# x's high part and residual side by side: 512-column matmuls in the first block's feature slots

## The chip, the cores and the metric

The kernel runs on one NeuronCore of a Trainium2 chip, in one launch. The metric is the time of that launch on the device, in microseconds (us).
TensorE multiplies matrices: a block of up to 128x128 values stands still in the array (the weight load), and a moving operand of up to 512 columns is streamed past it; the result goes to PSUM, which has 8 banks of 512 float32 columns. ScalarE computes functions of one value (sigmoid, exp, copies), VectorE arithmetic on one or two tensors, GpSimd the same more slowly, and SyncE issues the DMAs. Each engine runs its own instructions in order and waits on semaphores for the others.

## The reference

Three blocks are computed in float32 on x of 256 tokens (T) by 2048 features: one of the first kind, which this change concerns, and two of a second kind. The first block:

```python
xn = rms_norm(x, norm_pre_w)
z = xn @ w_in                       # split in 8: u_lru, g_lru, q, k, v, g_attn, m_lru, m_attn
u = centred_depthwise_conv(u_lru, conv_w, conv_b)             # 4 taps
h = rg_lru(u, ..., reverse=False) + rg_lru(u, ..., reverse=True)
y_a = h * silu(g_lru)
y_b = windowed_gqa(partial_rope(q), partial_rope(k), v, sink) * silu(g_attn)
merged = sigmoid(m_lru) * (y_a @ w_proj_a) + sigmoid(m_attn) * (y_b @ w_proj_b)
x = x + rms_norm(merged @ w_out, norm_post_w)
# rg_lru: gate_r, gate_i = sigmoid(u @ w_r + b_r), sigmoid(u @ w_i + b_i) per block of 128 features,
# a = exp(-8 gate_r softplus(-lam)), h[t] = a[t] h[t-1] + sqrt(1 - a^2)[t] gate_i[t] u[t]
```

## The kernel before, in words

**Products in three terms.** TensorE's fast float32 format (fp32r) keeps fewer bits. Each operand is therefore held as a high part (rounded to the format) and a residual (the value less the high part), and a product is the sum hi*hi + hi*lo + lo*hi. For x these are `xn_hi` and `xn_lo`, two tensors of [128, 16 k-tiles, 256 tokens] (line 2955); for the weights, `w_hi` and `w_lo`.

**The ring of slots** (class `Ring`, line 246). The weights come as slots of 128 x 2048 values (1 MB), numbered in order of use. SyncE loads slot n into one of two raw buffers (`load`, 254; it waits until the slot two before it has been split). ScalarE rounds it to `w_hi` (`round`, 263; 4 buffers, so it also waits until slot n-4 has been used), and VectorE subtracts to get `w_lo` (`residual`, 272). TensorE then uses it, and `used` counts the slots done.

**Feature slots** (`features`, 297) give one tile of 128 features by 256 tokens: for each of 16 k-tiles the weights stand still and x moves, three matmuls of 256 columns, 48 a slot. The result fills half a PSUM bank, `tile(b)` (444). **Token slots** (`tokens`, 309) keep x still and stream 512 weight columns, 24 matmuls a slot.

**The first block's slots.** 0 to 31: eight passes of the LRU branch, four feature slots each (two of `u_lru`, into banks `z[0]` and `z[1]`, then two of `g_lru`, into `z[2]` and `z[3]`). 32 to 39: keys and values (token slots). 40 to 71: four attention chunks, each of four token slots (queries) and four feature slots (`g_attn`), so there are 48 feature slots. Then come token slots only.

**A pass i of the LRU branch.** TensorE runs slots 4i to 4i+3 and then the gate products `gates(i)` (1108): eight float32 products with the convolved u, two PSUM banks a feature tile. The other engines go through iterations 0 to 8 (lines 605 and 872); iteration i handles the inputs of pass i and the gates of pass i-1, with n = 4i. The order in each engine is the order of the program:

- ScalarE: `gate_inputs(i-1)` (556: sigmoid of `g_lru`), `gates(i-1)` (563: eight sigmoids of the gate products), round n+3, `tanhs(i-1)`, round n+4, `input_copy(i)` (593: PSUM to `padded`), `exps_lru(i-1)` with a square root, round n+5, round n+6, `round_y(i-1)` (601), which waits for `y`.
- VectorE: `open_gates(i-1)` (839: `g_lru` times its sigmoid, which also frees its bank), residual n+3, residual n+4, `convolve(i)` twice (825: four taps each), `scan(i-1)` (844), residual n+5, `outputs_lru(i-1)` (860: makes `y`), residual n+6, `split_y(i-1)`.
- GpSimd multiplies `gate_i` by u when the eight sigmoids are done.
- TensorE waits, ahead of slot 4i+b, for `input_copy(i-1, b)`, and ahead of slot 4i+2+b for `open_gates(i-1)`; ahead of `gates(i)` for the convolution and for the sigmoids of the pass before.

Iteration 0 has VectorE's softplus chain of small instructions at its end, iteration 2 the rotary angles.

**An attention chunk c.** After the query slots ScalarE copies them out and VectorE rotates them; TensorE transposes heads and computes scores between the four feature slots, VectorE (`soften`, 933) and ScalarE (`exps`) form the softmax in the same stretch, and ScalarE's `silu(c, j)` (665) takes feature slot j out of PSUM. TensorE waits for the `silu` two before to reuse a bank (1206 to 1210). The chunk's end is done during the next one (`finish_chunk`).

Of the kernel before, what the change touches and what calls it, by code (L numbers as in the profile page):

```python
# [245 lines left out]
class Ring:  # L246
# [61 lines left out]

    def tokens(self, pe, n, quarter, outs, x_hi, x_lo):
# [36 lines left out]
def reduce_angles(link, dve, angle, turns, rest, looked):  # L346
# [4 lines left out]
    for n, quarter in enumerate((0.0, 0.25)):  # L351
# [5 lines left out]
        for m, part in enumerate(turn_parts):  # L357
# [8 lines left out]
           "weights0 weights1 gated cleared chain exped ucopied conv gsig zcopied gates taken decay dsteps rounded_y ydone "  # L366
           "counted rotary_in rchain rlooked mask_in sink_in sinkready "
           "kcopied kroped kturned keyed vcopied qcopied roped qturned qevac scored0 scored1 soft0 soft1 "
           "exped0 exped1 flipped0 flipped1 fcopied0 fcopied1 mixed0 mixed1 yout0 yout1 yrounded0 yrounded1 ylo silued "
# [4 lines left out]
def first_block(k, t):  # L374
# [3 lines left out]
    with phase(nc, "b1", B1_SEMS) as s:  # L378
# [67 lines left out]

        def pair(c):
            return (z[2 * (c % 2)][:, 0:Q], z[2 * (c % 2) + 1][:, 0:Q])
# [10 lines left out]
        with nc.Block() as block:  # L459
# [55 lines left out]
            def _(act):  # L515
                act.wait_ge(s.eps, 1)
                act.activation(k.warm[:], k.eps[:], ACT.Sqrt)
                for h in range(2):
                    for m in range(2):
                        act.wait_ge(x_in[2 * m + h], 16)  # L520
                        act.activation(k.junk[:, half(m, m)], x_first[:, m, half(m, h)], ACT.Square, scale=D ** -0.5,
                                       accum_out=k.squares[:, m, h:h + 1]).then_inc(s.squared, 1)
# [142 lines left out]
                def silu(c, j):  # L665
# [3 lines left out]
                    act.activation(gate[:, j], tile(2 + j % 2), ACT.Silu).then_inc(s.silued, 1)  # L669

                def finish_chunk(c, n):

                    ring.round(act, n + 3)
# [3 lines left out]
                    if c >= 0:  # L677
                        copy_weights(c, 0)
                        silu(c, 3)
# [8 lines left out]
                for c in range(4):  # L688
# [10 lines left out]
                    for h in range(2):  # L699
                        act.wait_ge(s.qturned, 2 * c + h + 1)  # L700
                        act.activation(q_turned[:, 2 * h:2 * h + 2], both(aux[2 + h]), ACT.Copy).then_inc(s.qevac, 1)
                    ring.round(act, n + 8)
                    silu(c, 0)
                    ring.round(act, n + 9)
                    silu(c, 1)
                    silu(c, 2)
# [68 lines left out]
            def _(dve):  # L775
# [96 lines left out]
                for i in range(LRU_PASSES + 1):  # L872
                    n = 4 * i
                    if i:
                        open_gates(i - 1)
# [9 lines left out]
                    if i:  # L885
                        scan(i - 1)
# [74 lines left out]

                def open_heads(c, p):
# [10 lines left out]
                def finish_chunk(c, n):  # L973
                    if c >= 0:
                        normalise(c, 0)
                    ring.residual(dve, n + 3)
# [13 lines left out]
                for c in range(4):  # L990
# [5 lines left out]
                    ring.residual(dve, n + 7)  # L996
                    ring.residual(dve, n + 8)
                    soften(c, 0)
                    ring.residual(dve, n + 9)
                    soften(c, 1)  # L1000
                    ring.residual(dve, n + 10)
# [81 lines left out]
            def _(pe):  # L1083
# [41 lines left out]

                for i in range(LRU_PASSES):
                    for b in range(2):
                        if i:
                            pe.wait_ge(s.ucopied, 2 * (i - 1) + b + 1)
                            ring.features(pe, 4 * i + b, tile(b), k.xn_hi, k.xn_lo)  # L1130
                        else:
                            ring.features(pe, b, tile(b), k.xn_hi, k.xn_lo, (first_rows, second_rows)[b], False)
# [1932 lines left out]
```

## Time and profile before

| | |
|---|---|
| median of 3 runs | 1992.32 us (1991.84 to 1992.9) |
| the profiled execution | 1995.17 us, its span 1993.4 us |
| TensorE busy | 1935.8 us (97%), 13840 matmuls |
| VectorE busy | 1265.2 us (63%) |
| ScalarE busy | 1104.7 us (55%) |
| mean granted TensorE clock | 0.996 of full speed |
| feature matmuls of 256 columns (line 306, all three blocks) | 3 x 2112 |
| token matmuls of 512 columns (line 318, weights moving) | 3 x 568 with xn, 3 x 368 with y |

The span is the time between the first and the last instruction; the metric has 1.8 us more around it. Times in a view count from the start of the span. A busy share is an average over the whole program; what one stage is bound by is read from the waits and the order of events in that stage. A matmul's recorded duration is longer than the distance between two starts, since matmuls overlap in the array: distances of starts are what they cost.

### The profile page before, as it was taken

The page shows a single profiled execution, that of the slowest core. Times are in us where ns is not written, and L with a number is a line of the kernel's source. Part 1 is how long each engine was busy: PE and PEld are TensorE (multiplying, and loading weights), DVE is VectorE, ACT ScalarE, POOL GpSimd, SP SyncE. Part 2 cuts the span into 40 slices and gives each one's busy share as a digit, 9 for nine tenths or more (in the row PEclk, how much of TensorE's full clock was granted, in tenths as well). Part 3 has the DMA queues.
Part 4 walks back from the last instruction along what each step waited for, and adds up shares of the span by engine and source line. Part 5 has one row for each costly group of instructions (what it writes and reads, how often), then busy time and mean ns, then how long its engine had stood idle before and what let it go on. Part 6 is the DMA issues. An engine that isn't in the chain of part 4 may idle for free.

```text
span 1993.4 us, 32637 instructions
## 1 busy us (share of the span) xinstructions
PE 1935.8 (97%) x13840; PEld 1726.6 (87%) x13840; DVE 1265.2 (63%) x1771; ACT 1104.7 (55%) x1506; POOL 70.1 (4%) x66
## 2 busy tenths in 40 slices
PE   6999999999999999999899999999999999999998
PEld 6999989999888888888798988888889998988887
DVE  5878755555444434654587987555557899775453
ACT  6777745554433333334556578826455656883451
POOL 0111100000000000000000011100000001010000
PEclk9999999999999999999999999999999999999999
DMA  6444454444455555464544343312555444342154
GB/s 226 183 183 183 166 205 160 161 152 143 175 175 205 190 187 190 178 250 169 208 172 149 146 166 112 141 70 104 212 194 208 168 157 140 128 148 86 64 191 148
DMA packets 52272, 328.61 MB, mean 165 GB/s; under 512 B 7968, under 2 KB 10144, under 8 KB 14368
## 3 DMA queue, kind: packets, MB, share of 16 engines
q1 hardware_dynamic: 52128, 326.54, 45.5%
q8 instruction: 109, 1.79, 0.3%
q14 instruction: 35, 0.29, 0.1%
HBM read 320.23 MB, written 6.29 MB: 164 GB/s over the span
## 4 chain that ended last, share of the span: by engine, by line
PE 26%; DVE 11%; ACT 8%; DMA 5%; issue 2%; SPq 0%; DVEq 0%; ACTq 0%
PE z L306 13%; DMA w_raw<-in_w_dram 5%; DVE w_lo L277 4%; PE z L318 4%; ACT w_hi L270 3%; PE aux L2683 2%; DVE acc L2006 2%; DVE conv L2164 1%; PE z L342 1%; PE aux L2592 1%; PE aux L2688 1%; PE z L2521 1%; DVE S L2120 0%; PE aux L2767 0%; DVE S L2145 0%
## 5 line engine op out<-in xcount | busy, mean ns | idle before, releaser
L277 DVE TENSOR_TENSOR w_lo<-w_raw,w_hi 128x2048 fp32r<-128x2048 f32 x274 | 631.3, 2305 | 445.2 <-ACT w_hi L270 444.6
L270 ACT ACTIVATE w_hi<-w_raw 128x2048 fp32r<-128x2048 f32 x286 | 548.1, 1918 | 506.2 <-PE z L318 246.5
L306 PE MATMUL z<-xn_hi,w_hi 128*128 128x256 f32 x2112 | 621.7, 294 | 2.7 <-DVE xn_lo L234 1.5
L306 PE MATMUL z<-xn_hi,w_lo 128*128 128x256 f32 x2112 | 596.4, 282 | 0.0
L306 PE MATMUL z<-xn_lo,w_hi 128*128 128x256 f32 x2112 | 595.6, 282 | 0.0
L306 PEld LDWEIGHTS z<-xn_hi,w_hi 128*128 128x128 f32 x2112 | 398.8, 189 | 22.3 <-issue 13.4
L306 PEld LDWEIGHTS z<-xn_lo,w_hi 128*128 128x128 f32 x2112 | 399.5, 189 | 5.0 <-issue 4.3
L306 PEld LDWEIGHTS z<-xn_hi,w_lo 128*128 128x128 f32 x2112 | 397.9, 188 | 0.0
L318 PE MATMUL z<-w_hi,xn_hi 128*128 128x512 f32 x568 | 226.9, 399 | 0.0
L318 PE MATMUL z<-w_lo,xn_hi 128*128 128x512 f32 x568 | 225.2, 396 | 0.0
L318 PE MATMUL z<-w_hi,xn_lo 128*128 128x512 f32 x568 | 225.1, 396 | 0.0
L318 PE MATMUL z<-w_hi,y_hi 128*128 128x512 f32 x368 | 143.6, 390 | 0.0
L318 PE MATMUL z<-w_hi,y_lo 128*128 128x512 f32 x368 | 143.3, 389 | 0.0
L318 PE MATMUL z<-w_lo,y_hi 128*128 128x512 f32 x368 | 143.2, 389 | 0.0
L318 PEld LDWEIGHTS z<-w_hi,xn_lo 128*128 128x128 f32 x568 | 107.0, 188 | 26.1
L318 PEld LDWEIGHTS z<-w_hi,xn_hi 128*128 128x128 f32 x568 | 107.0, 188 | 25.4
L318 PEld LDWEIGHTS z<-w_lo,xn_hi 128*128 128x128 f32 x568 | 107.0, 188 | 25.3
L2006 DVE SCALAR_TENSOR_TENSOR acc<-padded_b,params,acc 128x256 f32<-128x256 f32 x240 | 98.5, 478 | 0.0
L318 PEld LDWEIGHTS z<-w_hi,y_lo 128*128 128x128 f32 x368 | 69.1, 188 | 14.3
L318 PEld LDWEIGHTS z<-w_hi,y_hi 128*128 128x128 f32 x368 | 69.1, 188 | 14.2
L2164 DVE SCALAR_TENSOR_TENSOR conv<-padded,params,conv 128x256 f32<-128x256 f32 x108 | 58.1, 538 | 36.7 <-ACT conv L1738 34.1
L318 PEld LDWEIGHTS z<-w_lo,y_hi 128*128 128x128 f32 x368 | 69.1, 188 | 14.1
(428 smaller groups left out, 2527.9 us busy)
## 6 DMA issues: line engine op xcount, KB each, us to landing
w_raw<-in_w_dram SPq DMA_DIRECT2D x287, 1024.0 KB, 4.8
gate_w<-in_lru_w_dram SPq DMA_DIRECT2D x8, 512.0 KB, 5.6
x_t<-state_dram SPq DMA_DIRECT2D x2, 2048.0 KB, 8.3
x_first<-in_x_dram SPq DMA_DIRECT2D x4, 512.0 KB, 6.5
x_t<-in_x_dram SPq DMA_DIRECT2D x1, 2048.0 KB, 10.6
state_dram<-x_t SPq DMA_DIRECT2D x2, 1024.0 KB, 5.3
pw<-in_pw_dram SPq DMA_DIRECT2D x2, 1024.0 KB, 6.6
state_dram<-x_t SPq DMA_DIRECT2D x8, 256.0 KB, 2.3
```

The costliest lines, as they stand in the source:

```text
L270: act.activation(self.k.w_hi[:, n % SLOTS], self.k.w_raw[:, m % RAW], ACT.Copy).then_inc(self.s.rounded, 1)
L277: dve.tensor_tensor(self.k.w_lo[:, n % SLOTS], self.k.w_raw[:, m % RAW], self.k.w_hi[:, n % SLOTS].bitcast(F32), ALU.subtract).then_inc(se ...
L306: ins = pe.matmul(out, w[:, kk], x[:, kk], start=kk == 0 and j == 0, stop=kk == KT - 1 and j == 2)
L318: ins = pe.matmul(outs[m], x[:, row, t], w[:, kk], start=row == 0 and j == 0, stop=row == KT - 1 and j == 2)
L342: ins = pe.matmul(outs[m], x[:, row, t], w[:, kk], start=row == 0 and j == 0, stop=row == KT - 1 and j == 2)
L2006: dve.scalar_tensor_tensor(out=acc[:, b], in0=padded_b[:, b, n:n + T], scalar=col(w), in1=acc[:, b], op0=ALU.mult, op1=ALU.add).then_inc(s ...
L2164: dve.scalar_tensor_tensor(out=conv[:, i], in0=padded[:, i, tap:tap + T], scalar=col(w), in1=conv[:, i], op0=ALU.mult, op1=ALU.add).then_i ...
L2521: ins = pe.matmul(z[3][0:2 * H, 0:T], w[:, kk], x[:, kk], start=kk == 0 and i == 0, stop=kk == KT - 1 and i == 2)
L2592: ins = pe.matmul(aux[m // 2][:, T * (m % 2):T * (m % 2) + T], pw[:, b, P * m:P * m + P], wide[:, b], start=b == 0, stop=b == B - 1)
L2683: ins = pe.matmul(block(bank, h, hf), left[part_of(hf), h], right[part_of(hf), h], start=True, stop=True)
L2688: ins = pe.matmul(block(bank, h, hf), x[part_of(hf), h], ident_c[part_of(hf)], start=True, stop=True)
```

## The change

Three things change together.

1. `xn_hi` and `xn_lo` become views of one tensor `xn` of [128, 16, 2, 256], so that for each k-tile the high part and the residual of x lie side by side. In the 48 feature slots of the first block, `wide_features` streams both in one matmul of 512 columns against `w_hi`, into a whole bank, and then 256 columns of the high part against `w_lo`, into the bank's first half: 32 matmuls a slot. The bank then holds hi*hi + lo*hi in its first half and hi*lo in the second (`rest`).
2. The two halves have to be added. ScalarE copies the first half out (`take_gates`, `take_gate`, the `input_copy` that was there), VectorE adds the second half from PSUM (`join_gates`, `join_gate`, a join at the head of `convolve`), and sigmoid and silu read the sum in SBUF. TensorE waits for the joins where it waited for the copies.
3. TensorE's `gates(i)` moves from the end of pass i into the first slot of pass i+1, ahead of its seventh k-tile (for the last pass, behind the first key slot). ScalarE's sigmoids move behind round n+3, VectorE's `open_gates` from the head of the iteration to between the convolution and the scan.

`junk` and `x_whole`, scratch that lies in the same memory, get the same interleaved form. The two blocks behind use the old `features` on the new layout.

```diff
+    def wide_features(self, pe, n, bank, x, each=None, whole=True):
+        w_hi, w_lo = (w[:, n % SLOTS].rearrange("p (k f) -> p k f", k=KT) for w in (self.k.w_hi, self.k.w_lo))
+        out = bank[:, 0:2 * T]
+        if whole:
+            self.await_slot(pe, n)
+        for kk in range(KT):
+            if each is not None:
+                each(kk)
+            row = x[:, kk].rearrange("p b t -> p (b t)")
+            if kk < KT - 1:
+                pe.matmul(out, w_hi[:, kk], row, start=kk == 0, stop=False)
+            ins = pe.matmul(out[:, 0:T], w_lo[:, kk], x[:, kk, 0], start=False, stop=False)
+            if kk == KT - 1:
+                ins = pe.matmul(out, w_hi[:, kk], row, start=False, stop=True)
+        ins.then_inc(self.s.used, 1)
...
+                def take_gates(i):                                        # ScalarE
+                    act.wait_ge(s.used, 4 * i + 4)
+                    if i:
+                        act.wait_ge(s.dsteps, 8 * i)
+                    for b in range(2):
+                        act.activation(g_all[:, b], tile(2 + b), ACT.Copy).then_inc(s.gtaken, 1)
                 def gate_inputs(i):
-                    act.wait_ge(s.used, 4 * i + 4)
                     if i:
                         act.wait_ge(s.zcopied, 2 * i)
                     for b in range(2):
-                        act.activation(gsig[:, b], tile(2 + b), ACT.Sigmoid).then_inc(s.gsig, 1)
+                        act.wait_ge(s.gjoined, 2 * i + b + 1)
+                        act.activation(gsig[:, b], g_all[:, b], ACT.Sigmoid).then_inc(s.gsig, 1)
...
                     if i:
-                        gate_inputs(i - 1)
-                        gates(i - 1)
+                        take_gates(i - 1)
                     ring.round(act, n + 3)
                     if i:
+                        gates(i - 1)
+                        gate_inputs(i - 1)
                         tanhs(i - 1)
...
-                def silu(c, j):
+                def take_gate(c, j):
                     act.wait_ge(s.used, SLOT_ATT + 8 * c + 4 + j + 1)
                     if c:
                         act.wait_ge(yout[j // 2], c)
-                    act.activation(gate[:, j], tile(2 + j % 2), ACT.Silu).then_inc(s.silued, 1)
+                    act.activation(gate[:, j], tile(2 + j % 2), ACT.Copy).then_inc(s.ataken, 1)
+                def silu(c, j):
+                    act.wait_ge(s.ajoined, 4 * c + j + 1)
+                    act.activation(gate[:, j], gate[:, j], ACT.Silu).then_inc(s.silued, 1)
...
                 def convolve(i, b):                                       # VectorE
                     dve.wait_ge(s.ucopied, 2 * i + b + 1)
+                    inner = padded[:, b, 2:2 + T]
+                    dve.tensor_tensor(inner, rest(b), inner, ALU.add).then_inc(s.ujoined, 1)
+                    dve.wait_ge(s.ujoined, 2 * i + b + 1)
...
+                def join_gates(i):
+                    for b in range(2):
+                        dve.wait_ge(s.gtaken, 2 * i + b + 1)
+                        dve.tensor_tensor(g_all[:, b], rest(2 + b), g_all[:, b], ALU.add).then_inc(s.gjoined, 1)
                 def open_gates(i):
                     dve.wait_ge(s.gsig, 2 * i + 2)
+                    dve.wait_ge(s.gjoined, 2 * i + 2)
                     for b in range(2):
-                        dve.tensor_tensor(g_all[:, b], tile(2 + b), gsig[:, b], ALU.mult).then_inc(s.zcopied, 1)
+                        dve.tensor_tensor(g_all[:, b], g_all[:, b], gsig[:, b], ALU.mult).then_inc(s.zcopied, 1)
...
                     if i:
-                        open_gates(i - 1)
+                        join_gates(i - 1)
                     ring.residual(dve, n + 3)
...
                         convolve(i, 1)
                     if i:
+                        open_gates(i - 1)
                         scan(i - 1)
...
+                def join_gate(c, j):
+                    dve.wait_ge(s.ataken, 4 * c + j + 1)
+                    dve.tensor_tensor(gate[:, j], rest(2 + j % 2), gate[:, j], ALU.add).then_inc(s.ajoined, 1)
...
+                def last_gates(kk, i):                                    # TensorE
+                    if kk == 6:
+                        gates(i)
...
-                            pe.wait_ge(s.ucopied, 2 * (i - 1) + b + 1)
-                            ring.features(pe, 4 * i + b, tile(b), k.xn_hi, k.xn_lo)
+                            pe.wait_ge(s.ujoined, 2 * (i - 1) + b + 1)
+                        if i:
+                            ring.wide_features(pe, 4 * i + b, z[b], k.xn, None if b else lambda kk: last_gates(kk, i - 1))
...
-                            pe.wait_ge(s.zcopied, 2 * (i - 1) + b + 1)
-                        ring.features(pe, 4 * i + 2 + b, tile(2 + b), k.xn_hi, k.xn_lo)
-                    gates(i)
-
-                pe.wait_ge(s.ucopied, 2 * LRU_PASSES)
+                            pe.wait_ge(s.gjoined, 2 * (i - 1) + b + 1)
+                        ring.wide_features(pe, 4 * i + 2 + b, z[2 + b], k.xn)
+                pe.wait_ge(s.ujoined, 2 * LRU_PASSES)
                 for w in range(4):
                     ring.tokens(pe, SLOT_K + w, w, pair(0), k.xn_hi, k.xn_lo)
+                    if w == 0:
+                        gates(LRU_PASSES - 1)
...
-        k.xn_hi, k.xn_lo = (put(n, [P, KT, T], F32R) for n in ("xn_hi", "xn_lo"))
+        k.xn = put("xn", [P, KT, 2, T], F32R)
+        k.xn_hi, k.xn_lo = k.xn[:, :, 0], k.xn[:, :, 1]
```

In the attention chunks ScalarE's `take_gate(c, j)` stands where `silu(c, j)` stood or ahead of the next round (j = 3 moves to the head of `finish_chunk`), silu 0 and 1 follow round n+9, silu 2 and 3 follow `copy_weights(c, 0)`; VectorE's `join_gate` stands behind residual n+7, `soften(c, 0)`, `soften(c, 1)` and `normalise(c, 0)`. TensorE waits for the joins.

## Rows read from the trace of the kernel before

**Rows 1.** Waits, 0 to 262 us: who waited for whom, total us, times, longest.

```profile
PE aux L1116 <- DVE u_all L835: 1.5, 1, 1.5
ACT y_hi L603 <- DVE y L865: 34.2, 7, 5.0
```

**Rows 2.** Timeline, TensorE, pass 1's end: start, us, instruction, operands.

```profile
65.80 0.28 PE L306 MATMUL z<-xn_lo,w_hi 128*128 128x256 f32 x1
...
71.80 3.62 PE L1116 MATMUL aux<-u_all,gate_w 128*128 128x256 f32 x16
75.07 0.47 PE L306 MATMUL z<-xn_hi,w_hi 128*128 128x256 f32 x1
```

**Rows 3.** Timeline, TensorE, in value slot 37.

```profile
263.19 0.39 PE L318 MATMUL z<-w_hi,xn_hi 128*128 128x512 f32 x1
...
268.11 0.38 PE L1149 MATMUL aux<-ident,q_tok 128*128 128x128 f32 x2
```

**Rows 4.** Timeline, TensorE, the gate products of pass 7.

```profile
230.92 3.62 PE L1116 MATMUL aux<-u_all,gate_w 128*128 128x256 f32 x16
```

**Rows 5.** Timeline, ScalarE, iteration 4, and two later roundings of y; idle in brackets.

```profile
133.29 0.63 ACT L603 ACTIVATE y_hi<-y 128x512 fp32r<-128x512 f32 x1 [5.03 <-DVE y L865]
133.94 1.28 ACT L561 ACT_TABLE_LOAD   x1
...
143.83 0.71 ACT L599 ACTIVATE padded<-z 128x256 f32<-128x256 f32 x2
144.56 1.28 ACT L588 ACT_TABLE_LOAD   x1
...
148.88 1.06 ACT L591 ACTIVATE tau<-tau 128x1024 f32<-128x1024 f32 x1
...
158.57 0.63 ACT L603 ACTIVATE y_hi<-y 128x512 fp32r<-128x512 f32 x1 [5.04 <-DVE y L865]
...
183.86 0.63 ACT L603 ACTIVATE y_hi<-y 128x512 fp32r<-128x512 f32 x1 [4.50 <-DVE y L865]
```

**Rows 6.** Timeline, VectorE, iteration 4.

```profile
135.98 0.75 DVE L842 TENSOR_TENSOR g_all<-z,gsig 128x256 f32<-128x256 f32 x2
140.64 2.94 DVE L277 TENSOR_TENSOR w_lo<-w_raw,w_hi 128x2048 fp32r<-128x2048 f32 x1 [3.91 <-ACT w_hi L270]
...
146.24 0.41 DVE L831 TENSOR_SCALAR u_all<-padded,params 128x256 f32<-128x256 f32 x1
146.68 1.53 DVE L835 SCALAR_TENSOR_TENSOR u_all<-padded,params,u_all 128x256 f32<-128x256 f32 x3
148.12 0.41 DVE L831 TENSOR_SCALAR u_all<-padded,params 128x256 f32<-128x256 f32 x1
...
150.01 1.22 DVE L848 SCALAR_TENSOR_TENSOR tau<-decay,tau 128x1024 f32<-128x1024 f32 x1
```

**Rows 7.** Timelines, iterations 0 and 1 (VectorE, ScalarE), and the DMA issues.

```profile
45.08 2.28 DVE L277 TENSOR_TENSOR w_lo<-w_raw,w_hi 128x2048 fp32r<-128x2048 f32 x1
...
59.33 1.71 ACT L581 ACTIVATE tau<-gate_r,scale_t 128x256 f32<-128x256 f32 x4 [3.18 <-DVE scale_t L906]
...
62.75 0.63 ACT L599 ACTIVATE padded<-z 128x256 f32<-128x256 f32 x2
...
w_raw<-in_w_dram SPq DMA_DIRECT2D x287, 1024.0 KB, 4.8
```

**Rows 8.** Timelines, iteration 8 and the keys: VectorE, ScalarE, VectorE.

```profile
255.44 2.27 DVE L277 TENSOR_TENSOR w_lo<-w_raw,w_hi 128x2048 fp32r<-128x2048 f32 x1
...
259.14 0.63 ACT L603 ACTIVATE y_hi<-y 128x512 fp32r<-128x512 f32 x1 [4.88 <-DVE y L865]
...
263.22 0.29 DVE L922 TENSOR_TENSOR q_tok<-rope_a,rope_b 128x128 f32<-128x128 f32 x1
```

**Rows 9.** Stretch of 48 us in the attention chunks (engine busy, count), and VectorE's softmax start.

```profile
358.00:406.00 48.00, 48.00 (x315) 43.94 (x314) 27.48 (x41) 26.19 (x41) 0.00 (x0) 1.00 0.46 166
...
317.03 1.29 DVE L936 SCALAR_TENSOR_TENSOR S<-aux,mask 128x512 f32<-128x512 f32 x2 [2.71 <-PE aux L1164]
```

More of the change, by code:

```diff
@@ L445, in tile, with rest @@
             return z[n][:, 0:T]
+        def rest(n):
+            return z[n][:, T:2 * T]
         def pair(c):
@@ L520, in _ @@
                         act.wait_ge(x_in[2 * m + h], 16)
-                        act.activation(k.junk[:, half(m, m)], x_first[:, m, half(m, h)], ACT.Square, scale=D ** -0.5,
+                        act.activation(k.junk[:, 4 * m:4 * m + 4], x_first[:, m, half(m, h)].rearrange("p (j t) -> p j t", t=T), ACT.Square, scale=D ** -0.5,
                                        accum_out=k.squares[:, m, h:h + 1]).then_inc(s.squared, 1)
@@ L678, in finish_chunk @@
                         copy_weights(c, 0)
+                        silu(c, 2)
                         silu(c, 3)
@@ L701, in _ @@
                         act.activation(q_turned[:, 2 * h:2 * h + 2], both(aux[2 + h]), ACT.Copy).then_inc(s.qevac, 1)
+                    take_gate(c, 0)
                     ring.round(act, n + 8)
+                    take_gate(c, 1)
+                    ring.round(act, n + 9)
                     silu(c, 0)
-                    ring.round(act, n + 9)
                     silu(c, 1)
-                    silu(c, 2)
+                    take_gate(c, 2)
                     ring.round(act, n + 10)
@@ L975, in finish_chunk @@
                         normalise(c, 0)
+                        join_gate(c, 3)
                     ring.residual(dve, n + 3)
@@ L996, in _ @@
                     ring.residual(dve, n + 7)
+                    join_gate(c, 0)
                     ring.residual(dve, n + 8)
                     soften(c, 0)
+                    join_gate(c, 1)
                     ring.residual(dve, n + 9)
                     soften(c, 1)
+                    join_gate(c, 2)
                     ring.residual(dve, n + 10)
@@ L1151, in turn_heads @@
                             ins.then_inc(out_sem, 1)
-                pe.wait_ge(s.zcopied, 2 * LRU_PASSES)
+                pe.wait_ge(s.gjoined, 2 * LRU_PASSES)
                 for w in range(4):
@@ L1208, in _ @@
                         else:
-                            pe.wait_ge(s.silued, 4 * c + j - 1)
-                        ring.features(pe, n + 4 + j, tile(2 + j % 2), k.xn_hi, k.xn_lo)
+                            pe.wait_ge(s.ajoined, 4 * c + j - 1)
+                        ring.wide_features(pe, n + 4 + j, z[2 + j % 2], k.xn)
                         if j == 0:
@@ L1225, in _ @@
                     if c == 1:
-                        pe.wait_ge(s.silued, 16)
+                        pe.wait_ge(s.ajoined, 16)
                     elif c:
@@ L1607, in scalar @@
             after(act, s.squared_x, since.squared_x + m)
-            act.activation(k.junk[:, 0:Q if layer else D], x, ACT.Square, scale=D ** -0.5, accum_out=total).then_inc(s.squared_x, 1)
+            act.activation(k.junk[:, 0:2 if layer else D // T], x.rearrange("p (j t) -> p j t", t=T), ACT.Square, scale=D ** -0.5, accum_out=total).then_inc(s.squared_x, 1)
         act.wait_ge(s.averaged, since.averaged + 1)
@@ L1929, in square @@
                 act.wait_ge(s.added, since.added + 2 * c + m + 1)
-                act.activation(k.junk[:, (2 * c + m) % 4 * Q:(2 * c + m) % 4 * Q + Q], x_t[:, m, cols(c)], ACT.Square, scale=D ** -0.5,
+                here = slice(2 * ((2 * c + m) % 4), 2 * ((2 * c + m) % 4) + 2)
+                act.activation(k.junk[:, here], x_t[:, m, cols(c)].rearrange("p (j t) -> p j t", t=T), ACT.Square, scale=D ** -0.5,
                                accum_out=k.squares[:, m, c:c + 1])
@@ L2954, in build @@
         k.middle = goto(k.xn_at)
-        k.xn_hi, k.xn_lo = (put(n, [P, KT, T], F32R) for n in ("xn_hi", "xn_lo"))
+        k.xn = put("xn", [P, KT, 2, T], F32R)
+        k.xn_hi, k.xn_lo = k.xn[:, :, 0], k.xn[:, :, 1]
         goto(k.xn_at)
-        k.junk = put("junk", [P, D])
-        goto(k.xn_at + 4 * KT * T)
-        k.x_whole = put("x_whole", [P, KT, T])
+        k.junk = put("junk", [P, KT, 2, T])[:, :, 0]
+        goto(k.xn_at)
+        k.x_whole = put("x_whole", [P, KT, 2, T])[:, :, 1]
         k.raw_at = k.middle + 4096
```

8 lines of the change are left out of this document (5 added, 3 removed).

## The prediction

> **What bounds the kernel now.** I read the page's busy times first: TensorE is busy 97% of the span, so the time moves only if TensorE's instructions get shorter or its waits change. Next I read the waits of the stage that the change touches, up to 262 us. Once TensorE has its first slots it waits there once, for 1.5 us, before the first pass's gate products [rows 1]; in the passes and in the attention chunks it runs without a gap. ScalarE, however, waits in seven of the eight iterations for `y` of VectorE, 34.2 us in all [rows 1]. Two clocks run side by side. TensorE's passes come every 26.5 us: the gate products of pass 1 start at 71.80 and those of pass 7 at 230.92, six passes in 159.1 [rows 2, 4]. ScalarE and VectorE hand work back and forth in a closed loop, from one rounding of `y` to the next: 133.29 to 158.57 is 25.28 us, and to 183.86 it is 25.29 again [rows 5]. That loop is only 1.2 us shorter than TensorE's pass. This margin decides the case.
>
> **The matmuls.** In a feature slot, 50 matmuls of 256 columns take from 65.80 to 71.80, 0.120 us apart [rows 2]; in a token slot, 21 of 512 columns take from 263.19 to 268.11, 0.2343 apart [rows 3]. A slot is 48 x 0.120 = 5.76 us now. Changed it is 16 x (0.2343 + 0.120) = 5.67, so 0.09 less. The column count (12,288) is unchanged and only 16 starts disappear. Bounds: no gain if the columns of a feature slot cost what they do now; 0.13 us if all run at the token slots' rate (12,288 x 0.2343/512 = 5.62). I take 0.09. For 48 slots that is 4.3 us at most.
> The Trainium skill (TensorE: Matmul & The Clock Gate, "Wait — 56ns, not 53.3ns?") speaks against more: a matmul costs its columns plus some 2.5 ns, so 16 fewer starts would be an estimate of 0.04 us a slot, under 2 us for 48. The measured starts differ by 2 x 120 - 234.3 = 5.7 ns, more than that, and the sum goes by the rows.
>
> **The gate products** cost 3.27 us before and after (71.80 to 75.07 [rows 2]); they only move to the seventh k-tile of the next pass's first slot. TensorE's own pass becomes 26.5 - 4 x 0.09 = 26.1 us. The four slots of pass 0 save nothing, as their ends hang on the first splits.
>
> **The ScalarE/VectorE loop, where the price is.** Its legs now [rows 5, 6]: ScalarE from rounding `y` (133.29) through table load, two sigmoids of the gate input, eight gate sigmoids, round of slot n+3, tanhs and round of slot n+4 to 143.83; VectorE's residual of slot n+4, 2.4 with its hand-over; the convolution 146.24 to 150.01, 3.77 us; scans, residual n+5, outputs, and back to ScalarE at 158.57, 8.56 us. The order inside ScalarE's leg changes but its work stays (the same number of table loads, since Copy needs none). Added to the loop:
> - ScalarE's two copies of the gate input (`take_gates`): as the two `padded` copies, 143.83 to the next start at 144.56, 0.73; I take 0.72.
> - VectorE's two joins inside `convolve`, each followed by a wait for itself. The nearest are the two `g_all` multiplies, same operands, 0.75 for both [rows 6], so 0.34 a start without a wait, and the three waited taps, 146.68 to 148.12, 0.48 each. I take 0.45 each, 0.90.
> - `open_gates`, moved from the stretch in which VectorE then idled 3.91 us [rows 6] to between convolution and scan: two multiplies, 0.70 (0.62 to 0.75).
> - The joins of the gate inputs take the old place of `open_gates`, in that idle stretch: nothing, while VectorE waits there for ScalarE.
> Could the ScalarE side hide VectorE's 1.60? Its decays and square root run 143.83 to 149.94 (148.88 + 1.06 [rows 5]), VectorE reaches the scan at 150.01. The two legs are level already, so all of VectorE's addition lands. The loop becomes 25.28 + 0.72 + 0.90 + 0.70 = 27.6 us (bounds 27.2 to 27.8), against TensorE's 26.1. So the loop, which lagged nobody, sets the pace: TensorE will wait 1.5 us in every pass.
>
> **Adding it up.** Iteration 1 is special: its tanhs wait for VectorE's softplus chain until 59.33, and round n+4 ends at 62.75 [rows 7]. In the changed order the sigmoids come behind round n+3, which needs slot 7, whose load needs slot 5's residual: 45.08, plus two joins 0.9, plus 2.2 of residual, plus 4.8 of load [rows 7] is 53.0. From there the same five items as in ScalarE's leg (133.94 to 143.83, 9.9 us [rows 5]) lead to 62.9; its tanhs then start near 59.5, so the chain no longer matters. With 0.90 and 0.70 behind it, the `y` of iteration 1 is 1.8 late (1 to 3). Iterations 2 to 7 add 2.3 each, 13.9. Iteration 8 has no convolution and waits for the square root, so it adds only the copies, 0.7. The last `y`, now at 259.14, comes 16.4 later, at 275.5.
> What TensorE needs from it [rows 8]: the residual of slot 37 ends (255.44 + 2.2) 1.5 before the last `y`, so at 274.0, and slot 37 (5.63) ends at 279.6. The rotated keys, now done at 263.5, 4.4 after the last `y`, come at 279.9, and the key transposes start then, where they started at 268.11. TensorE is 11.8 us late. The other 4.6 of the 16.4 are slack that the keys have now (263.5 to 268.11). Nothing behind gives it back, for TensorE runs there without gaps.
> In the attention chunks ScalarE is busy 26.2 and VectorE 27.5 us of 48 [rows 9]. Four copies and four joins a chunk (3 us) fit. The tightest is the second join, behind `soften`: that starts at 317.03 with 1.29 us for two products [rows 9] and a reduction over their results, an estimate of 3 us; the slot that reuses the bank starts a whole slot, 5.7 us, after the scores. If one were late, it costs tenths. So the 16 gate slots there give their 16 x 0.09 = 1.4 us.
> The strided halves of `xn`, `junk` and `x_whole` keep runs of 256 columns and change no count; I cost them at nothing (VectorE and ScalarE have idle time; each full pass over `xn` is a few instructions).
> Sum: +11.8 - 1.4 = +10.4. The profiled execution took 1995.17 (span 1993.4 and 1.8 around it), so 2005.6; the median of the runs is 2.85 lower, so **2002.7 us**.
>
> **Rivals.**
> - *TensorE keeps the pace (faster).* It wins if the loop grows by less than about 0.8 us a pass: 1.2 of margin, and the starting slack, cover that. The joins and `open_gates` would have to hide. For it: TensorE's passes have no gap now, and round n+3 now comes ahead of the sigmoids, some 4 us sooner after `y`. Against: that round stays in ScalarE's leg, only its place changes. Price: 44 x 0.09 = 4.0, plus the 1.5 before the first gate products: 1992.3 - 5.4 = 1986.9. Chance 0.08.
> - *Only ScalarE's copies lengthen the loop* (VectorE's additions fall beside decays that prove slower from the new order). Loop 26.0, level with TensorE: the last `y` is some 5 late (7 x 0.72), the slack takes 4.6, TensorE is about 1 late, and the attention slots give 1.4: 1992. Against: the two legs end 0.07 apart. Chance 0.07.
> - *More than the loop.* TensorE now stops inside an open slot for the convolution (the gate products' wait) and ends late; if its late slots then hold the rounds (which wait for a used slot) the two add up instead of overlapping, 1 us a pass more: 2010. Against: with the loop in the lead, round n+4 finds its slot free 14 us early. Chance 0.05.
> - *The wide matmul is no cheaper than its columns* (no gain in the attention slots): 2004.1. This lies inside the forecast's own spread.
>
> **How the numbers follow.** The forecast has 0.80. Its own range: 0.25 us a pass on six passes, 1 us of iteration 1, 1.4 of the matmuls, 1999 to 2006. A measurement of this kernel tells 0.2% (4 us) from nothing. The middle rival and the small edge of the forecast give "within" 0.09, the first rival gives "faster" 0.08, the rest is slower, 0.83. The range for 8 in 10 takes in the forecast with both bounds of the prices and a little on the low side: 1997 to 2008.
>
> **What would show it.** In the changed profile: wide matmuls 0.234 and narrow 0.120 apart, slots 5.67; roundings of `y` 27.6 us apart in iterations 3 to 7, with no idle time on VectorE between convolution, `open_gates` and scan; TensorE waiting once or twice a pass, for `w_lo` of slot 4i+5 (behind the scan) and for the convolution inside slot 4i+4, 1.5 us together; the gate products of successive passes 27.6 apart; the key transposes near 280; from there on, TensorE 12 to 10 us behind the old times. I am wrong if passes stay 26.1 apart, if ScalarE reaches the square root later than VectorE the scan, or if the attention chunks show new waits.

## The result, and the profile after

The changed kernel takes 2018.26 us (median of 4 runs, 2017.18 to 2021.67) against 1992.61 for the kernel before in the same comparison (1991.84 to 1993.7). The ratio is 1.0121, with a 95% interval of 1.0109 to 1.0134: slower by 25.7 us (the quotient of the two medians, 1.0129, lies inside the interval). The forecast, 2002.7 us, had the direction, but its increase was 10.4, and the time lies 10 us above its range. The profiled execution took 2021.67 us with a span of 2019.9, 26.5 more than the span before.

Each fence below is from the changed kernel unless its sentence says otherwise. The page's busy times first (share of the span, and number of instructions):

```profile
PE 1946.7 (96%) x13072; PEld 1695.4 (84%) x13072; DVE 1276.6 (63%) x1819; ACT 1116.7 (55%) x1538; POOL 69.5 (3%) x66
```

TensorE has 768 matmuls fewer and is yet busy 10.9 us longer than before, at a mean granted clock of 0.988 against 0.996; and the time in which it does nothing grew from 57.6 to 73.2 us. The waits of TensorE up to 300 us, which answer to [rows 1] (who waited for whom: us in total, times, longest; the 12.8 us until the first x is there, 12.9 before, are left out):

```profile
PE aux L1171 <- DVE u_all L875: 8.4, 6, 2.0
PE z L335 <- DVE w_lo L277: 5.4, 2, 4.3
PE z L320 <- DVE g_all L882: 2.7, 1, 2.7
PE z L320 <- DVE w_lo L277: 2.2, 3, 1.1
PE z L335 <- DVE padded L865: 2.0, 1, 2.0
PE z L320 <- DVE padded L865: 1.1, 2, 0.6
```

L1171 is the gate products, now inside a slot, and they wait for the convolution as forecast. The same view of ScalarE, 0 to 300 us:

```profile
ACT y_hi L630 <- DVE y L911: 44.2, 7, 6.6
ACT w_hi L270 <- DMA w_raw<-in_w_dram: 33.6, 15, 4.5
```

Before, the second row read 20.7 us in 11 waits in the same window. That row is the part that the forecast did not have. The timeline of ScalarE over one iteration shows where it sits (start, duration, instruction; in brackets the idle time before it and what ended it). It answers to [rows 5]:

```profile
171.62 0.63 ACT L630 ACTIVATE y_hi<-y 128x512 fp32r<-128x512 f32 x1 [6.61 <-DVE y L911]
172.16 0.64 ACT L581 ACTIVATE g_all<-z 128x256 f32<-128x256 f32 x2
174.96 1.92 ACT L270 ACTIVATE w_hi<-w_raw 128x2048 fp32r<-128x2048 f32 x1 [2.16 <-DMA w_raw<-in_w_dram]
176.89 1.28 ACT L596 ACT_TABLE_LOAD   x1
...
183.28 1.95 ACT L270 ACTIVATE w_hi<-w_raw 128x2048 fp32r<-128x2048 f32 x1
185.09 0.68 ACT L626 ACTIVATE padded<-z 128x256 f32<-128x256 f32 x2
...
190.11 1.06 ACT L618 ACTIVATE tau<-tau 128x1024 f32<-128x1024 f32 x1
...
201.40 0.64 ACT L630 ACTIVATE y_hi<-y 128x512 fp32r<-128x512 f32 x1 [6.62 <-DVE y L911]
```

From one rounding of `y` to the next is 29.78 us, not 27.6. Behind the two copies of the gate input ScalarE stands still for 2.16 us: the round of slot n+3 at 174.96, which the change put ahead of the sigmoids, has no data yet. VectorE's timeline over the same stretch (answers to [rows 6]) shows why:

```profile
167.93 2.27 DVE L277 TENSOR_TENSOR w_lo<-w_raw,w_hi 128x2048 fp32r<-128x2048 f32 x1
170.11 0.68 DVE L908 TENSOR_TENSOR gate_r<-gate_r 128x512 f32<-128x512 f32 x1
170.90 0.69 DVE L911 TENSOR_TENSOR y<-gate_r,g_all 128x512 f32<-128x512 f32 x1
...
176.91 2.29 DVE L277 TENSOR_TENSOR w_lo<-w_raw,w_hi 128x2048 fp32r<-128x2048 f32 x1 [1.85 <-ACT w_hi L270]
185.26 2.29 DVE L277 TENSOR_TENSOR w_lo<-w_raw,w_hi 128x2048 fp32r<-128x2048 f32 x1 [6.06 <-ACT w_hi L270]
187.47 0.42 DVE L865 TENSOR_TENSOR padded<-z,padded 128x256 f32<-128x256 f32 x1
...
192.16 0.75 DVE L888 TENSOR_TENSOR g_all<-g_all,gsig 128x256 f32<-128x256 f32 x2
192.83 1.22 DVE L894 SCALAR_TENSOR_TENSOR tau<-decay,tau 128x1024 f32<-128x1024 f32 x1
```

The residual of slot n+1 at 167.93 is the last reader of one of the two raw buffers. The load of slot n+3 goes out when it ends: SyncE issues it at 170.22, and with the 4.8 us of a load [rows 7] it lands at 175.0. Before the change the same round stood behind the sigmoids, 5.3 us behind `y`, and found its data there. Everything else in the loop is as forecast: the convolution with its joins is 4.69 us (187.47 to 192.16), 0.92 more than before; `open_gates` holds VectorE 0.67; and VectorE has no gap from 185.26 to `y`.

Last, TensorE at the end of the stage, first the timeline, then granted clock and busy times by window (us, engines with their counts, PEclk, share and GB/s of the DMA); they answer to [rows 3, 8]:

```profile
284.24 0.39 PE L335 MATMUL z<-w_hi,xn 128*128 128x512 f32 x1
288.93 0.79 PE L335 MATMUL z<-w_hi,xn 128*128 128x512 f32 x1 [4.30 <-DVE w_lo L277]
289.52 0.63 PE L335 MATMUL z<-w_lo,xn 128*128 128x512 f32 x1
...
297.05 0.40 PE L335 MATMUL z<-w_hi,xn 128*128 128x512 f32 x1
297.29 1.03 PE L1210 MATMUL aux<-ident,q_tok 128*128 128x128 f32 x8
```

```profile
284.00:288.00 4.00, 0.63 (x3) 0.19 (x1) 3.97 (x6) 1.33 (x1) 0.00 (x0) 0.99 0.00 0
288.00:292.00 4.00, 3.07 (x7) 2.48 (x8) 3.90 (x4) 1.60 (x3) 0.00 (x0) 0.50 0.46 158
292.00:298.00 6.00, 6.00 (x25) 4.78 (x24) 4.90 (x11) 2.54 (x2) 0.00 (x0) 0.77 0.78 288
```

The last `y` is rounded at 290.31, 31.2 later than before. Slot 37 waits 4.30 us for its residual and then takes 8.36 us (288.93 to 297.29) where it took 5.63, because TensorE comes out of that wait at half clock (0.50 granted, the 1.2 GHz level). The key transposes start at 297.29, 29.2 later than before.

### The profile page after: what moved, and what is told of

Its sections match the earlier page's. It is cut to its first block, busy times and chain, and to the rows that moved or that the text cites. A ratio compares the mean times of both kernels' runs of the same rounds, so it can differ in the third digit from the quotient of the medians.

```text
span 2019.9 us, 31201 instructions
## 1 busy us (share of the span) xinstructions
PE 1946.7 (96%) x13072; PEld 1695.4 (84%) x13072; DVE 1276.6 (63%) x1819; ACT 1116.7 (55%) x1538; POOL 69.5 (3%) x66
## 4 chain that ended last, share of the span: by engine, by line
PE 27%; DVE 11%; ACT 7%; DMA 4%; issue 2%; SPq 0%; DVEq 0%; ACTq 0%
PE z L306 14%; DMA w_raw<-in_w_dram 4%; PE z L335 4%; DVE w_lo L277 4%; ACT w_hi L270 3%; PE aux L2745 2%; DVE acc L2068 2%; DVE conv L2226 1%; PE z L359 1%; PE aux L2654 1%; PE aux L2750 1%; PE z L2583 1%; DVE S L2207 0%; PE aux L2829 0%; DVE S L2182 0%
## 5 line engine op out<-in xcount | busy, mean ns | idle before, releaser
L306 PE MATMUL z<-xn,w_hi 128*128 128x256 f32 x2688 | 512.8, 290 | 2.0 <-DVE xn L234 2.0
L306 PEld LDWEIGHTS z<-xn,w_hi 128*128 128x128 f32 x2688 | 416.9, 189 | 25.4 <-issue 17.1
L306 PE MATMUL z<-xn,w_lo 128*128 128x256 f32 x1344 | 379.8, 283 | 0.0
L335 PE MATMUL z<-w_hi,xn 128*128 128x512 f32 x1136 | 367.3, 401 | 7.4 <-DVE w_lo L277 5.4
L320 PE MATMUL z<-xn,w_hi 128*128 128x512 f32 x720 | 262.5, 403 | 6.1 <-DVE g_all L882 2.7
L335 PEld LDWEIGHTS z<-w_hi,xn 128*128 128x128 f32 x1136 | 216.0, 190 | 60.6 <-DVE w_lo L277 4.7
L306 PEld LDWEIGHTS z<-xn,w_lo 128*128 128x128 f32 x1344 | 253.4, 189 | 0.0
L335 PE MATMUL z<-w_lo,xn 128*128 128x512 f32 x568 | 226.7, 399 | 0.0
L321 PE MATMUL z<-xn,w_lo 128*128 128x256 f32 x768 | 207.9, 281 | 0.0
L320 PEld LDWEIGHTS z<-xn,w_hi 128*128 128x128 f32 x720 | 136.2, 189 | 38.9 <-DVE g_all L882 3.1
L321 PEld LDWEIGHTS z<-xn,w_lo 128*128 128x128 f32 x768 | 145.3, 189 | 3.8
L335 PEld LDWEIGHTS z<-w_lo,xn 128*128 128x128 f32 x568 | 108.2, 190 | 25.7
```

What stands on the lines that cost most here:

```text
L306: ins = pe.matmul(out, w[:, kk], x[:, kk], start=kk == 0 and j == 0, stop=kk == KT - 1 and j == 2)
L320: pe.matmul(out, w_hi[:, kk], row, start=kk == 0, stop=False)
L321: ins = pe.matmul(out[:, 0:T], w_lo[:, kk], x[:, kk, 0], start=False, stop=False)
L335: ins = pe.matmul(outs[m], x[:, row, t], w[:, kk], start=row == 0 and j == 0, stop=row == KT - 1 and j == 2)
```

## The experiments

All are edits of the changed kernel unless said otherwise. "Late" is the start of the key transposes less the 268.11 of before [rows 3]; ratios are to the kernel before in the same comparison.

| run | ratio (95%) | roundings of `y` apart | last `y` | late |
|---|---|---|---|---|
| the change | 1.0121 (1.0109 to 1.0134) | 29.8 | 290.31 | 29.2 |
| e1 round n+3 behind the gates | 1.0056 (1.0041 to 1.0071) | 27.5 | 276.92 | 14.7 |
| e2 `open_gates` early | 1.0094 (1.0077 to 1.0111) | 29.1 | 286.42 | 24.2 |
| e3 gate products at pass end | 1.0112 (1.0097 to 1.0127) | 29.8 | 288.65 | 24.9 |
| e4 wide in attention only | 1.0003 (0.9991 to 1.0015) | 25.3 | 259.50 | 0.8 |
| e5 both orders | 1.0032 (1.0021 to 1.0042) | 26.8 | 272.91 | 9.1 |
| e6 no joins for the convolution | 0.9993 (0.9983 to 1.0003) | 25.9 | 266.72 | 4.5 |
| m1 convolution in the idle stretch | 1.0089 (1.0074 to 1.0104) | 30.2 to 30.6 and 26.2 to 27.2, in turn | 283.60 | 19.8 |
| m2 as m1, copies ahead of `y`'s rounding | 1.0093 (1.0078 to 1.0108) | 31 and 26, in turn | 285.25 | 21.5 |
| b1 wide for gate inputs only | 0.9982 (0.9973 to 0.9991) | 25.35 | 260.26 | -0.4 |
| b2 all wide, copies in idle time | 0.9997 (0.9988 to 1.0006) | 26.3 | 266.19 | 2.4 |

**e1: one line moved back.** My theory after seeing the trace: the early round of slot n+3 costs its wait for the load, in every iteration. The rival: this round is only where the delay shows, and the loop would be as long without it.

```
-                    ring.round(act, n + 3)
-                    if i:
                         gates(i - 1)
                         gate_inputs(i - 1)
+                    ring.round(act, n + 3)
+                    if i:
                         tanhs(i - 1)
```

> ScalarE's round of slot n+3 goes back behind the gate sigmoids and the sigmoid of the gate input; all else as changed. Theory A (the closed loop of ScalarE and VectorE sets the pace; the forecast missed that round n+3, now 1.3 us after y, meets a load that lands only 3.3 us after y, since the load waits for a residual that ends 1.5 us before y): roundings of y 27.6 us apart instead of 29.8, no wait of round n+3 for the DMA, last rounding near 276, key transposes near 280, time 2001 to 2004. Rival B (TensorE's own stops, above all the wait for the convolution inside an open slot and the lower clock behind it, carry the loss): at most 2 to 4 us gained, 2014 to 2018.

The loop fell to 27.48 us, the last `y` to 276.92 and the ratio to 1.0056; half of the loss is gone. ScalarE's timeline in e1:

```profile
168.40 0.63 ACT L630 ACTIVATE y_hi<-y 128x512 fp32r<-128x512 f32 x1 [6.47 <-DVE y L911]
168.94 0.64 ACT L581 ACTIVATE g_all<-z 128x256 f32<-128x256 f32 x2
169.60 1.28 ACT L596 ACT_TABLE_LOAD   x1
...
174.38 1.96 ACT L270 ACTIVATE w_hi<-w_raw 128x2048 fp32r<-128x2048 f32 x1
177.78 1.94 ACT L270 ACTIVATE w_hi<-w_raw 128x2048 fp32r<-128x2048 f32 x1
...
195.88 0.63 ACT L630 ACTIVATE y_hi<-y 128x512 fp32r<-128x512 f32 x1 [6.61 <-DVE y L911]
```

The round at 174.38, now 6.0 us behind the rounding of `y`, waits for nothing. The theory stands, and this kernel is close to the one that the forecast had priced (27.6; last `y` 275.5; transposes 279.9, measured 282.81). The time, 2007.25 us, is above the 2001 to 2004 expected: the transposes come 2.9 us later than priced, and slot 37 takes 7.27 us here instead of 5.63. One interval is 28.2; in it the round of slot n+4 waited 0.62 us for its load.

**e2: `open_gates` alone.** It tests the price of the moved multiplies, and whether VectorE's side sets the loop at all.

```
+                    if i:
+                        open_gates(i - 1)
                     ring.residual(dve, n + 4)
```

(and the call behind the convolution goes.)

> VectorE's open_gates ahead of residual n+4, in the stretch where it waits for ScalarE; all else as changed. Theory A: 0.67 us out of the loop in seven iterations, 29.1 apart, last rounding near 286, time 2013 to 2015. Rival B: y is not what the end hangs on, no change, 2017 to 2019.

The loop became 29.1, 0.7 less: the two multiplies count in full. But the kernel is still 1.0094, so this was not the large term.

**e3: the gate products back at the end of their pass.** The rival here was my own "more than the loop": TensorE stopping inside an open slot.

```
-                            ring.wide_features(pe, 4 * i + b, z[b], k.xn, None if b else lambda kk: last_gates(kk, i - 1))
+                            ring.wide_features(pe, 4 * i + b, z[b], k.xn)
...
                         ring.wide_features(pe, 4 * i + 2 + b, z[2 + b], k.xn)
+                    gates(i)
```

> TensorE's gate products back at the end of their own pass; all else as changed, wide slots and joins too. Theory A: the loop stays at 29.8, for the sigmoids of the gates come later than the products either way; TensorE waits 5 us a pass in one piece at the gate products instead of 2 us inside the slot; time 2018 to 2021. Rival B: without the stop inside the slot 8 us of waits go, 2008 to 2012.

TensorE's waits up to 262 us in e3:

```profile
PE aux L1171 <- DVE u_all L875: 18.3, 7, 3.8
PE aux L1148 <- DVE x_first L823: 12.8, 1, 12.8
```

The wait for the convolution grew from 8.4 to 18.3 us (at most 3.8 in one pass, where I expected 5), the loop stayed at 29.8, and the intervals of the two ratios overlap. Whoever follows a slower partner waits somewhere; the place of the gate products is worth little. Slot 37 of e3 starts behind a wait of 2.10 us and takes 5.72 us (287.28 to 293.00), and the granted clock there is 1.00:

```profile
287.00:293.00 6.00, 5.72 (x25) 4.58 (x25) 5.83 (x13) 2.63 (x4) 0.00 (x0) 1.00 0.73 258
```

So its transposes come 4.3 us before those of the change, though its last `y` comes only 1.7 before; the rest, 2.6, is the slow slot.

**e4: the attention chunks alone.** The LRU stage is computed as before, and the 16 gate slots of the attention stay wide.

```
-                        ring.wide_features(pe, 4 * i + 2 + b, z[2 + b], k.xn)
+                        ring.features(pe, 4 * i + 2 + b, tile(2 + b), k.xn_hi, k.xn_lo)
```

(the same for the input slots; copies, joins and orders of the LRU stage as before.)

> The wide slots only in the 16 feature slots of the attention chunks (with their copies and joins); the 32 feature slots of the LRU branch, their order and TensorE's gate products as before the change, on the interleaved x. Both theories: the loss lies wholly in the LRU branch, passes 26.5 apart, roundings of y 25.3 apart; the attention slots give 0.15 us each, 2.4 us, so 1989.5 to 1991 (same as before within the measurement). If the interleaved layout or the copies and joins cost something in the attention chunks or behind: above 1993.

1.0003 (0.9991 to 1.0015): all of the loss arises in the LRU stage. The times do not show the gain of 2.4 us (0.12%) that the wide slots should bring, but the traces do. Behind the attention chunks ScalarE's first sigmoid of `m_lru` waits for TensorE to end slot 75. Its row before, in the changed kernel and in e4:

```profile
522.99 1.09 ACT L714 ACTIVATE merged<-z 128x512 f32<-128x512 f32 x2 [2.96 <-PE z L318]
```

```profile
549.92 1.09 ACT L751 ACTIVATE merged<-z 128x512 f32<-128x512 f32 x2 [2.96 <-PE z L335]
```

```profile
521.53 1.09 ACT L743 ACTIVATE merged<-z 128x512 f32<-128x512 f32 x2 [2.96 <-PE z L335]
```

From the key transposes to this row it is 254.88 us before, 252.63 in the changed kernel and 252.64 in e4; in all eleven kernels with the wide slots it lies between 252.63 and 252.67. So sixteen wide slots with their copies and joins give 2.2 us, 0.14 a slot. In e4 the key transposes come 0.8 us late, since TensorE's first gate products already start at 46.19 instead of 45.21; what delays them was not looked into. That leaves 1.4 us net, which lies inside the interval.

**e5 and e6: the rest of the loop, term by term.** e5 joins the edits of e1 and e2. e6 takes the two joins away as well; it leaves out the product of u's input residual with the high part of the weights.

```
-                    inner = padded[:, b, 2:2 + T]
-                    dve.tensor_tensor(inner, rest(b), inner, ALU.add).then_inc(s.ujoined, 1)
-                    dve.wait_ge(s.ujoined, 2 * i + b + 1)
```

> Both edits at once: round n+3 behind the gate sigmoids, and open_gates ahead of residual n+4. Theory A (the prices in the loop add up): roundings of y 27.5 - 0.7 = 26.8 us apart, 1.55 above the old 25.3, last rounding near 272, key transposes near 278, 0.3 to 0.5% above before (1999 to 2003 where before is 1993 to 1994). Rival B: the two overlap, no better than the first alone (0.56% above).

> As the kernel with both orders, but the two joins at the head of the convolution are left out, so u lacks the product of its x residual (that part of the result is not computed); TensorE waits for ScalarE's copies of u. Theory A: 0.9 us out of the loop, 25.9 to 26.1 apart, level with TensorE's own pass of 4 x 5.61 + 3.4 = 25.9; key transposes 266 to 271; 0.0 to 0.2% below before. Rival B (the join is cheap, what costs is something else in the pass, as the lower clock behind TensorE's stops): stays 0.3% or more above before.

The loops are 29.8, 27.5 (e1), 26.8 (e5) and 25.9 (e6). The steps, 2.3, 0.7 and 0.9, are the wait for the load, `open_gates` and the two joins, each as its rows had it. What is left above 25.28 is the copies, 0.6. The time follows: 1.0121, 1.0056, 1.0032, 0.9993. In e6 the loop is level with TensorE's own pass with wide slots, 25.9, and the loss is gone. Its transposes, at 272.60, still come later than the 266 to 271 expected; slot 37 takes 7.25 us in e6 and 5.71 in e5, behind waits of 1.99 and 2.08.

**m1 and m2: the convolution in VectorE's idle stretch.** The hope was to keep every wide slot and hide the joins: ScalarE does the gates' sigmoids and the copies of `u`'s input ahead of round n+3, and VectorE runs `open_gates` and both convolutions ahead of the residual of slot n+3. m2 also gives the gate inputs' copies their own buffer, ahead of the rounding of `y`.

```
+                        open_gates(i - 1)
+                        if i < LRU_PASSES:
+                            convolve(i, 0)
+                            convolve(i, 1)
```

> A version that keeps every join: ScalarE copies u right behind the gate sigmoids, ahead of round n+3; VectorE then does open_gates and the convolution with its joins in the 6 us in which it waited for ScalarE, ahead of residuals n+3 and n+4. Theory A: only ScalarE's copies of the gate input lengthen the loop, 25.3 + 0.7 = 26.0 apart, level with TensorE; key transposes 266 to 270; 0.0 to 0.25% below before. Rival B (the wide slots cost more elsewhere): 0.2% or more above before.

> As the version before, and ScalarE's copies of the gate input go into a buffer of their own, ahead of the rounding of y, where ScalarE waits 5 us for VectorE. Theory A: nothing of the change is left in the loop (25.3), TensorE sets the pace: passes 25.9 to 26.0, key transposes 264 to 267 where they were at 268.1, 0.15 to 0.35% below before (3 to 7 us). Rival B: within 0.1% of the version before, for another wait (a bank, a slot's load) takes over.

Both missed: 1.0089 and 1.0093; m2's rival (no more than 0.1% from m1) holds. In m1's timelines, first VectorE's row of `open_gates`, then GpSimd's, then ScalarE's round that waits, then TensorE's:

```profile
176.07 2.44 DVE L891 TENSOR_TENSOR g_all<-g_all,gsig 128x256 f32<-128x256 f32 x2 [2.72 <-ACT gsig L588]
```

```profile
175.50 2.73 POOL L532 TENSOR_TENSOR gate_i<-gate_i,u_all 128x512 f32<-128x512 f32 x2 [27.14 <-ACT gate_i L598]
```

```profile
191.43 1.92 ACT L270 ACTIVATE w_hi<-w_raw 128x2048 fp32r<-128x2048 f32 x1 [4.16 <-DMA w_raw<-in_w_dram]
```

```profile
185.55 0.48 PE L320 MATMUL z<-xn,w_hi 128*128 128x512 f32 x1 [3.69 <-DVE w_lo L277]
```

The convolution went ahead of a residual, the residual frees a raw buffer, and so the next loads went out late: the same edge from residual to load to round that had hit the change. SyncE issues the load at 185.43, when the first of the two residuals behind the convolution ends; the round at 191.43 waits 4.16 us for it, and TensorE waits for `w_lo` 19.2 us in 6 waits up to 262. No run takes this edge out of m1, so its share of the loss is read from the trace alone. A second cost: the two multiplies of `open_gates`, 0.75 us elsewhere, took 2.44 beside GpSimd's products.

**b1 and b2: what the runs point to.** If the loop sets the pace, then only work that stays out of it may be added. b1 keeps the wide matmul for the gate inputs alone (16 slots here, 16 in the attention) and leaves the input slots, whose join lies in the convolution, as before. The gate products go back to the end of the pass, with the orders of e5; the gate inputs' copies go to a buffer of their own in ScalarE's wait for `y`. (In the diff, `take_gates` now stands ahead of the rounding of `y`; VectorE's joins of the gate inputs stand behind `split_y`.) b2 has the same copies but all 48 slots wide, with the joins and the inner gate products.

```
+        g_in = put("g_in", [P, 2, T])
...
+                    if i < LRU_PASSES:
+                        take_gates(i)
...
-                            ring.wide_features(pe, 4 * i + b, z[b], k.xn, None if b else lambda kk: last_gates(kk, i - 1))
+                            ring.features(pe, 4 * i + b, tile(b), k.xn_hi, k.xn_lo)
```

> Wide slots only for the gate inputs (16 in the LRU branch, 16 in attention); u's slots narrow and without joins; gate products at the pass's end; round n+3 behind the gate sigmoids; open_gates ahead of residual n+4; ScalarE's copies of the gate input in a buffer of their own, ahead of the rounding of y; the first join ahead of the softplus chain. Theory A (what is taken out of the loop costs nothing): roundings of y 25.3 apart as before the change, TensorE's pass 26.5 - 2 x 0.15 = 26.2, key transposes 265.5 to 267 (268.1 before), 32 x 0.15 = 4.8 us less in all, 0.15 to 0.3% below before. Rival B (moving things into idle stretches makes weight loads late, as it did when the convolution was moved): 0.1% or more above before.

> All 48 slots wide with every join, gate products inside the next pass as in the change; the other edits of the version before. Theory A: the convolution's joins alone stay in the loop, 25.3 + 0.9 = 26.2 against TensorE's 25.9 to 26.1, so roundings of y 26.2 apart, last one near 266 to 268, key transposes 270 to 273, 0.15% below to 0.1% above before. Rival B: as above, 0.3% or more above before.

b1 takes 1992.6 us against 1996.15 for the kernel before, ratio 0.9982 (0.9973 to 0.9991), over 11 and 21 runs: the only interval here that lies wholly below 1. b2 ties with the kernel before. From ScalarE's timeline of b1, then TensorE's:

```profile
159.42 0.64 ACT L631 ACTIVATE y_hi<-y 128x512 fp32r<-128x512 f32 x1 [4.49 <-DVE y L912]
...
179.65 0.64 ACT L582 ACTIVATE g_in<-z 128x256 f32<-128x256 f32 x2
184.77 0.63 ACT L631 ACTIVATE y_hi<-y 128x512 fp32r<-128x512 f32 x1 [4.49 <-DVE y L912]
185.42 1.28 ACT L597 ACT_TABLE_LOAD   x1
```

```profile
267.67 1.03 PE L1210 MATMUL aux<-ident,q_tok 128*128 128x128 f32 x8
```

The copies at 179.65 end before `y` is there, and the loop is 25.35, what it was before [rows 5]. The gain is 3.6 us (1.8 to 5.4); 32 slots at 0.15 are 4.8. The trace shows where it arises. The transposes at 267.67 miss the 265.5 to 267 expected: the passes are 26.33 us long instead of 26.52, which gives 1.1 in six, but the first gate products start 1.0 late, at 46.19 as in e4. So 0.4 us is gained up to the transposes, and 2.2 in the attention chunks.

## Why the prediction was right in direction and wrong in size

- **What bounds: right.** The loop between ScalarE and VectorE overtook TensorE's 26.1 us a pass and set the pace. e1, e5 and e6 shorten the loop in steps, and the time follows each.
- **The added terms: right.** Joins 0.92 (forecast 0.90), `open_gates` 0.67 (0.70), copies 0.64 (0.72). Iteration 1 gave 2.07 (1.8).
- **"The order inside ScalarE's leg changes but its work stays": the step that failed.** The work did stay. But I moved a round past eleven instructions at no cost, without counting what it waits for. The prediction had the parts: the residual of slot n+1 ends 1.5 us before `y`, a load takes 4.8; so the data of slot n+3 come 3.3 us behind `y`, and the round now wants them after 1.2. For iteration 1 the prediction even worked this edge out: the round of slot 7 at 53.0, measured 53.06. It did not do so for the iterations behind it. In iterations 2, 4, 5, 6 and 7 ScalarE waited 2.18, 1.83, 2.16, 2.24 and 2.12 us, 10.5 together; the roundings 1 to 7 moved apart by 24.5 instead of 13.9, 10.6 more. Iteration 3 is the check within the trace: there the sine and cosine hold `y` back until 114.32, the residual had ended at 108.5, and the round waited for nothing. Iteration 8 waited 3.84 (its load took about 6.4 us from issue to landing instead of 4.8; why is open). With the 0.3 of iteration 1 that is 14.8 us, the whole of 31.2 less 16.4.
- **The slot behind the stall: missed.** I had slot 37 at its old 5.63 us, ending at 279.6. It ran 8.36. So 279.6 + 14.8 + 2.7 gives 297.1; measured 297.29. The 4.30 us wait came before it, and the clock was 0.50 just behind it. In e1 slot 37 took 7.3 us behind a wait of 2.10 (granted clock 0.76 in 276 to 283), in e3 5.72 behind a wait of the same 2.10, at 1.00. Behind waits of 2.0 to 2.1 us slot 37 took 5.71 in e5 and 5.72 in b2, but 7.25 in e6, and behind 4.30 us in e2 it took 7.26. So the length of the wait alone does not say whether the clock falls; no run was made to find what does. In the passes the clock fell as well behind waits of about 2 us (granted 0.79 in 190 to 198), and behind one of 1.99 at 162.52 the gate products took 3.72 us against 3.62 without a wait. There TensorE had time, since the loop set the pace.
 The Trainium skill (TensorE: Matmul & The Clock Gate, "What's actually happening") says that the clock has two levels, 1.2 and 2.4 GHz, and falls to the lower when the array has been idle. The trace agrees: 512-column starts lay 0.43 us apart behind the wait and 0.234 later.
- **The matmuls: right in sign, small in size.** Thirteen k-tiles of a wide slot in the attention run from 353.45 to 358.01, 0.351 each, so a slot is 5.61 us, 0.15 under the old 5.76 (forecast 0.09). TensorE's timeline:

```profile
353.45 0.40 PE L320 MATMUL z<-xn,w_hi 128*128 128x512 f32 x1
353.69 0.28 PE L321 MATMUL z<-xn,w_lo 128*128 128x256 f32 x1
...
358.01 0.39 PE L320 MATMUL z<-xn,w_hi 128*128 128x512 f32 x1
```

 Sixteen such slots would give 2.4 us; the traces show 2.2 over the attention chunks (e4), where the forecast had 1.4.
 The Trainium skill (TensorE: Matmul & The Clock Gate, "Wait — 56ns, not 53.3ns?") would make it an estimate of 0.04 us a slot from the starts alone. The measured 0.15 (0.14 over the whole chunks) is more, and the measurement decides.
- **Attention chunks: right.** In a window of 48 us that answers to [rows 9] TensorE is busy throughout, at full clock, with VectorE 28.9 and ScalarE 27.3; TensorE has no wait from 300 to 490 us:

```profile
385.00:433.00 48.00, 48.00 (x253) 40.90 (x252) 28.91 (x45) 27.29 (x44) 0.00 (x0) 1.00 0.44 165
```

- **The rivals.** "TensorE keeps the pace" and "only the copies" fell with the 29.8 us loop. "More than the loop" named a total near the truth for a wrong reason: e3 removes its cause and the time stays.

Summed: the forecast's +10.4, +14.8 for the early round, +2.7 for the slow slot, less 0.8 for the cheaper slots of the attention (2.2 instead of 1.4), are +27.1, against 26.5 in the spans and 25.7 in the medians.

## What to carry to other kernels

When an instruction is moved earlier, compute when its input is there: follow it back to the buffer's last reader, add the load, and compare with the new place; "the same work in another order" is free only if every moved piece has its data. Two engines that hand work back and forth are a clock of their own; write its length beside that of the busiest engine, and let added work in only where the partner waits anyway, as b1 does. A stall at the end of such a stage can cost more than its length, by the slower work of TensorE behind it (2.7 us here).

## What was not expected of the hardware

- A matmul of 256 columns beside one of 512 adds 0.117 us (0.351 less 0.234), while in the old slots three of them lie 0.120 apart [rows 2]. What makes the 3 ns was not tried.
- VectorE beside GpSimd: the two multiplies took 2.44 us beside GpSimd's products in m1, 0.75 alone, and GpSimd's products took 2.73 there and 2.54 in the changed kernel, where VectorE was idle.
 The Trainium skill (SBUF — State Buffer, "Who interferes with whom") says that a VectorE instruction with two inputs in SBUF contends with a GpSimd one that reads SBUF, and calls the port pair that they share an exclusive lock. The trace agrees: VectorE's first product (176.07 to 177.07) ends 0.28 us behind GpSimd's first, its second (177.00 to 178.51) 0.28 us behind GpSimd's second.
